# Third layer: the epsilon of the tail queries is added to their squares by VectorE, not by a one-row product on TensorE

## The reference, cut to what matters

```python
def rms_norm_2(x, g):
    xf = x.astype(jnp.float32)
    y = xf * lax.rsqrt(jnp.mean(xf * xf, axis=-1, keepdims=True) + EPS)
    return (y * g.astype(jnp.float32)).astype(x.dtype)

q, k, v, qi, ki, wi = jnp.split(h @ w_in, list(A_SPLITS), axis=-1)
q = rope(rms_norm_2(q.reshape(B, T, A_Q_HEADS, HEAD_DIM), q_gain), cos, sin)
...
score = jnp.einsum('qh,qhs->qs', w_blk, jax.nn.relu(logits))
score = jnp.where(causal, score, -jnp.inf)
_, idx = lax.top_k(score, topk)
```

## Time and profile before

| what | value |
|---|---|
| three runs, median | 1284.07 us (1283.54 to 1284.81) |
| the profiled execution | 1283.08 us |
| its span | 1281.2 us |
| TensorE busy | 1259.3 us, 98% of the span |
| VectorE busy | 808.0 us, 63% |
| ScalarE busy | 738.5 us, 58% |
| granted TensorE clock | 1.00 |

### The profile page before, as it was taken

How to read it: one execution, slowest core, us unless ns; L and a number is a source line. 1 busy time by engine, 2 the same in 40 slices (tenths; PEclk the granted TensorE clock), 3 DMA queues, 4 the chain that set the end, 5 groups by cost and what they waited for, 6 DMA issues and landing times.

```text
span 1281.2 us, 28400 instructions
## 1 busy us (share of the span) xinstructions
PE 1259.3 (98%) x10337; PEld 1214.3 (95%) x10337; DVE 808.0 (63%) x1422; ACT 738.5 (58%) x1375; POOL 375.8 (29%) x416
## 2 busy tenths in 40 slices
PE   6999999999999999999999899999999999999999
PEld 6988999999988999999989599999999889999999
DVE  5687755556576655556699875554547666755444
ACT  6566766654456566665566854443436776544433
POOL 2011344411000244431243027770100220677100
PEclk9999999999999999999999999999999999999999
DMA  7542655566654465666455046556555443655654
GB/s 263 179 136 87 190 186 183 184 208 201 214 173 154 151 195 180 193 194 207 152 183 172 11 151 182 176 172 190 172 173 180 152 139 101 194 183 182 198 189 154
DMA packets 66503, 220.55 MB, mean 172 GB/s; under 512 B 9312, under 2 KB 13808, under 8 KB 66288
## 3 DMA queue, kind: packets, MB, share of 16 engines
q1 hardware_dynamic: 64080, 212.77, 52.4%
q10 hardware_dynamic: 2336, 6.58, 1.6%
HBM read 215.61 MB, written 1.08 MB: 169 GB/s over the span
## 4 chain that ended last, share of the span: by engine, by line
PE 74%; issue 10%; DVE 5%; ACT 5%; POOL 5%; DMA 1%; POOLq 0%; ACTq 0%; SPq 0%; DVEq 0%
PE bank L341 22%; PE bank L343 22%; PE bank L342 22%; DVE wlo L325 1%; POOL scratch L581 1%; POOL scratch L583 1%; ACT prob L968 1%; ACT whi L320 1%; POOL alo L585 1%; PE bank L930 1%; DVE scratch L571 1%; ACT ahi L556 1%; PE bank L915 1%; PE bank L912 1%; PE bank L355 1%
## 5 line engine op out<-in xcount | busy, mean ns | idle before, releaser
L325 DVE TENSOR_TENSOR wlo<-raw,whi 128x1024 fp32r<-128x1024 f32 (+1 forms) x394 | 484.0, 1229 | 163.1 <-ACT whi L320 162.1
L341 PE MATMUL bank<-uhi,whi 128*128 128x256 f32 (+1 forms) x1848 | 532.6, 288 | 11.2 <-DVE wlo L325 10.2
L343 PE MATMUL bank<-uhi,wlo 128*128 128x256 f32 (+1 forms) x1848 | 524.8, 284 | 0.0
L342 PE MATMUL bank<-ulo,whi 128*128 128x256 f32 (+1 forms) x1848 | 524.0, 284 | 0.0
L320 ACT ACTIVATE whi<-raw 128x1024 fp32r<-128x1024 f32 (+1 forms) x394 | 410.6, 1045 | 184.0 <-PE bank L343 175.4
L341 PEld LDWEIGHTS bank<-uhi,whi 128*128 128x128 f32 x1848 | 349.6, 189 | 19.4 <-issue 16.7
L343 PEld LDWEIGHTS bank<-uhi,wlo 128*128 128x128 f32 x1848 | 349.9, 189 | 0.0
L342 PEld LDWEIGHTS bank<-ulo,whi 128*128 128x128 f32 x1848 | 348.4, 189 | 0.5
L341 PE MATMUL bank<-ahi,whi 128*128 128x256 f32 (+1 forms) x1168 | 332.9, 285 | 0.4 <-DVE wlo L325 0.4
L343 PE MATMUL bank<-ahi,wlo 128*128 128x256 f32 (+1 forms) x1168 | 330.6, 283 | 0.0
L342 PE MATMUL bank<-alo,whi 128*128 128x256 f32 (+1 forms) x1168 | 330.3, 283 | 0.0
(11 more groups left out here) (286 smaller groups left out, 1240.6 us busy)
## 6 DMA issues: line engine op xcount, KB each, us to landing
raw<-stream SPq DMA_DIRECT2D x394, 512.0 KB, 3.7
scratch<-decay ACTq DMA_DIRECT2D x8, 416.0 KB, 3.7
scratch<-relh ACTq DMA_DIRECT2D x8, 384.0 KB, 3.5
scratch<-scratch SPq DMA_DIRECT2D x68, 34.0 KB, 2.5
constants<-consts SPq DMA_DIRECT2D x1, 1296.0 KB, 11.4
h<-xT SPq DMA_DIRECT2D x4, 256.0 KB, 5.6
out<-h SPq DMA_DIRECT2D x8, 128.0 KB, 3.4
scratch<-scratch SPq DMA_DIRECT2D x16, 16.0 KB, 3.0
```

Of the source, the lines that this page charges most:

```text
L325: dve.tensor_tensor(wlo[:, s, 0:w], raw[:, s, 0:w], whi[:, s, 0:w].bitcast(F32), ALU.subtract).then_inc(w_lo, 1)
L341: pe.matmul(dst, hi, a, start=first and i == 0, stop=False)
L342: pe.matmul(dst, hi, b, start=False, stop=False)
L343: mm = pe.matmul(dst, lo, a, start=False, stop=last and i == chunks - 1)
```

## The change

In each of the eight dq units' statistics the one-row product L1814 is taken out, and L1813 closes the sum alone. Instead VectorE adds the scaled epsilon, spread over all 128 partitions, to the squares of the 16 tail columns in `ysq` before TensorE sums them (the matrix `headones` averages in such a way that this is the same number). This is the new function `tail_epsilon(i)`, one `tensor_tensor` of 128 x 16, with a new semaphore `y_eps`; TensorE waits for it between L1810 and L1813. On VectorE it stands in iteration i + 1 of the loop, behind `split_lo` and `second(i - 1)` and ahead of the top-k steps; for unit 19 it stands behind the first two heads' maxima. To have the number on all partitions, a product of a row of ones with the row of token factors is added once where wi is turned (`second` of wi on TensorE), one VectorE copy of 128 x 16 with it (`wi_done` now reaches 4), and the exponential L1979 works on 128 x 16 instead of 1 x 16.

```diff
                     elif name == "wi":
-                        pe.wait_ge(wi_done, 3)
+                        pe.wait_ge(wi_done, 4)
...
                     for t in range(2):
                         pe.matmul(st[:, 288 + 2 * t:290 + 2 * t], sq[:, 128 * t:128 * t + 128], const("headones")[:, 0:128:64],
                                   start=True, stop=True, skip_group_check=True)
-                    pe.wait_ge(q_eps, 2)
-                    pe.matmul(st[:, 292:308], const("headones"), sq[:, 256:T], start=True, stop=False, skip_group_check=True)
-                    pe.matmul(st[:, 292:308], ones[0:1, :], wi[0:1, 28:44], start=False, stop=True,
+                    pe.wait_ge(y_eps, j + 1)
+                    pe.matmul(st[:, 292:308], const("headones"), sq[:, 256:T], start=True, stop=True,
                               skip_group_check=True).then_inc(y_stat, 1)
...
-                        mm = pe.transpose(dsa_bank(i)[:, 24 + t:25 + t], x2_t[0:1, 2, 128 * t:128 * t + 128], const("ident")[0:1, 0:1])
-                    mm.then_inc(wi_turned, 1)
+                        pe.transpose(dsa_bank(i)[:, 24 + t:25 + t], x2_t[0:1, 2, 128 * t:128 * t + 128], const("ident")[0:1, 0:1])
+                    pe.matmul(dsa_bank(i)[:, 26:42], ones[0:1, :], x2_t[0:1, 2, 256:T], start=True, stop=True,
+                              skip_group_check=True).then_inc(wi_turned, 1)
...
-                act.activation(wi[0:1, 28:44], x2_t[0:1, 2, 256:T], ACT.Exp, bias=bias[0:1, 3:4]).then_inc(q_eps, 1)
+                act.activation(wi[:, 28:44], wi[:, 28:44], ACT.Exp, bias=bias[:, 2:3]).then_inc(q_eps, 1)
...
+            def tail_epsilon(i):
+                j, r = DSA[i][1], rms_of(i)
+                if j == 0:
+                    dve.wait_ge(q_eps, 2)
+                dve.wait_ge(y_sq, r + 1)
+                e = ysq[:, r % 2, 256:T]
+                dve.tensor_tensor(e, e, wi[:, 28:44], ALU.add).then_inc(y_eps, 1)
...
+                    dve.tensor_copy(wi[:, 28:44], dsa_bank(i)[:, 26:42]).then_inc(wi_done, 1)
...
                 if i >= 2 and DSA[i - 2][0] != "dk":
                     second(i - 2)
+                if i >= 1 and DSA[i - 1][0] == "dq":
+                    tail_epsilon(i - 1)
...
                     for i in (2 * s, 2 * s + 1):
                         biased_max_dve(dve, a, i)
+                if s == 0:
+                    tail_epsilon(19)
                 if s in (0, 4):
                     tail_max_dve(dve, s // 4)
```

More of the change, by code:

```diff
@@ L303, in program @@
         f_exp, f_log = sems("f_exp f_log")
-        q_tables, q_neg, q_eps = sems("q_tables q_neg q_eps")
+        q_tables, q_neg, q_eps, y_eps = sems("q_tables q_neg q_eps y_eps")
         t_q, t_s, t_max, t_exp, t_p, t_pt, t_pts, t_o, t_ohi, t_olo = sems(
@@ L1975, in epsilons @@
             def epsilons():
-                act.wait_ge(wi_done, 3)
+                act.wait_ge(wi_done, 4)
                 act.activation(wi[:, 26:28], wi[:, 24:26], ACT.Exp, bias=bias[:, 2:3]).then_inc(q_eps, 1)
-                act.activation(wi[0:1, 28:44], x2_t[0:1, 2, 256:T], ACT.Exp, bias=bias[0:1, 3:4]).then_inc(q_eps, 1)
+                act.activation(wi[:, 28:44], wi[:, 28:44], ACT.Exp, bias=bias[:, 2:3]).then_inc(q_eps, 1)
             for i in range(len(DSA)):
```

## The result

The changed kernel takes 1289.62 us, the median of 5 runs (1288.72 to 1291.12), against 1284.07 us before: the ratio is 1.0041, with a 95% interval of 1.0028 to 1.0054. Once more, in another session, it took 1289.83 us (10 runs) against 1284.63 us (33 runs), ratio 1.0039 (1.0026 to 1.0051). It is slower by 5.2 to 5.6 us as medians go.

A forecast was written before the change was run, and what follows sets the result against it. TensorE bounds the dq units, VectorE having 1.6 us spare in 32. Delay is +3.50 us at dq0, +4.38 through the ring, +3.52 at the next product, +4.6 after dq7: 1284.07 to 1288.7 us, range 1286.4 to 1290.8.

The forecast's parts named there:

- TensorE sets the pace: In the dq units TensorE is busy for all of 32.00 us, VectorE for 30.38; period 4.12 us, 3.80 without L1814.
- L1814's time is on the path: In the dq units, removing eight L1814 of 0.32 us takes 2.6 us off the path.
- The preparation is hidden: At wi, the additional product, some 0.3 us, fits in TensorE's 0.52 us idle time ahead of the first index product.
- VectorE reaches dq0's place over 3 us late: At dq0, TensorE reaches L1813 at 682.09, VectorE the addition's place at 685.30: a stall of over 3 us.
- X12: Start of L1813's weight load in dq0: 682.09 before, 685.59 forecast (+3.50 us).
- The ring at 4.28 us: Behind dq0, the loop L1813, L1926, L320, L325, addition, next L1813: 4.18 us plus 0.10 for each stall.
- 0.10 us for a product that starts on an idle TensorE: At each stall, a product on idle TensorE takes longer, as L1810 takes 0.61 instead of 0.50 us.
- my marks: Forecast starts of L1813's weight load by unit: 685.59 at dq0, 689.87, 694.39, 698.67, 702.95 at dq4, 710.65 at dq6.
- dq7's place costs 1.3 us: At unit 19, the addition behind L959's first two heads' maxima adds about 1.3 us, bringing the delay to +4.62 us.
- The clock stays up: At dq0's stall, the forecast counted no clock fall; the rival with a fall had chance 0.12.
- The rival's 1.7 us: Clock falls in first stall: 1.7 us more at dq1, 1.1 us stays; +5.7 us, 1289.8 us; chance 0.12.
- forecast 4.6: At the attention's start, total delay of +4.6 us, carried to the end: median 1284.07 to 1288.7 us; chance 0.60.

The follow-up runs named there:

- filler kernel: Changed kernel plus 13 float32 products of 128 x 128 constants on TensorE ahead of the wait at dq0 only: 1288.62 us, ratio 1.0031.
- Early: Changed kernel with the additions moved in VectorE's order to just behind the time their squares are there: 1282.29 us, again 1281.85 us (ratio 0.9979).
- early2: Early with dq6's and dq7's additions moved further up in VectorE's order: 1283.45 us (ratio 0.9989), again 1283.06 us (0.9987).
- one line up: Changed kernel with the addition ahead of `split_lo` in the same iteration, dq7's place kept: 1287.03 us against 1284.84, ratio 1.0007.
- late7: early2 with dq7's addition behind the first two heads' maxima, as in the change: 1283.71 us, ratio 0.9988.

## Why the prediction was right, and where it was off

- **TensorE sets the pace, and L1814's time is on the path:** right. A product's worth was 0.43 us instead of the 0.32 that I read off the chain and the weight loads, so a period paced by TensorE is 3.69 and not 3.80 us.
- **The preparation is hidden:** shown. The wider exponential takes 0.30 us, as the narrow one before took 0.29.
- **VectorE reaches dq0's place over 3 us late:** right, and the reason for the sign. Expected X12 was 685.59; less the 1.17 us of offset the profile has 685.54. The stall was 3.29 us (expected some 3.3). From the end of the addition to the waiting L1813 it is 0.06 us (686.65 to 686.71), where I had put 0.05.
- **The ring at 4.28 us:** shown. dq3 and dq4 follow at 4.29 and 4.30 us, and moving the addition past one instruction makes it 3.69. One term is right by luck. I added 0.10 us for a product that starts on an idle TensorE, read off L1810 at 709.11, but that one follows on L915 with no idle time ahead of it. In the turn of the ring above L1813 to L1926 is 0.43 us, with nothing to add, and the 0.10 us lies between the end of ScalarE's L320 and VectorE's L325 (699.62 to 699.73), where I had 0.01. In the filler kernel, where the clock doesn't fall, my marks hold: counted on the times of before, dq1 to dq4 lie at 689.84, 694.27, 698.57 and 702.87 against 689.87, 694.39, 698.67 and 702.95 predicted. Behind them it runs ahead of my sum, 710.27 against 710.65 at dq6: 0.11 us a period by the first point; it was 0.08 us ahead at dq4 already, and the 0.10 us of idle start isn't there (the period behind the last wait is 3.71 us, 0.02 over 3.69).
- **dq7's place costs 1.3 us:** 65.32 - 60.87 = 4.45 behind, after 3.13 at the tail's scores: 1.32 us.
- **The clock stays up:** this is the step that failed. I gave its fall a chance of 0.12, since no row showed a gap of that length, and a price of 1.1 us. It falls in both traces of the changed kernel, to 0.50 around gaps of 3.29 and 3.27 us, and costs 1.8 us. The rival's 1.7 us were my estimate, 17 x 0.10 us, from the kernel's start, where products follow each other 0.21 to 0.22 us apart from 10.55 to 14.18 us and 0.12 us apart later. No run shows that term behind a stall; here 21 or 22 of a unit's 24 are slow, and dq1's L1813 comes at 691.67 (692.84 less the offset) instead of the rival's 691.2. The ring then carries the delay on undiminished, where I had it shrink to 1.1 us.
- **The size:** at the turn the loss is 5.92 us, made of 4.14 us with the clock up (forecast 4.6; the product's higher worth and the idle start that isn't there explain the difference, about half each) and 1.78 us for the clock. The medians give 5.2 to 5.6 us. That the forecast, 1288.7 us, came within about 1 us of the result is in part luck: these two terms hid some 0.5 us of the missing 1.8 us for the clock.
- **By the busy shares of the whole kernel,** TensorE 98% and VectorE 63%, the sum would have been the removed products alone, -2.6 us. Early (-2.1 and -2.8 us), early2 (-1.4 and -1.6) and the additions on GpSimd (-1.9) show that they point the right way, once the engine that takes the work over is there in time; by themselves they say nothing of that.

What stays open: early's median is 1.2 us under early2's in the session that had both, its turn only 0.4 us earlier. How often the clock falls in the attention (below) may be the rest, but no run tells it apart.

## What to carry to other kernels

Before work goes from a full engine to a half-empty one, look at the time at which the other engine's queue reaches the place, not at its busy share: VectorE was 3.3 us behind TensorE here and nobody had noticed, since nothing waited. The wait that closed a ring over three engines cost 0.6 us in each turn here (4.29 us against 3.69); moving it ahead of the one instruction that closes the ring took 3.5 us off, 1.9 of them the ring's. And a stall of TensorE is dearer than its length when the clock falls in it or behind it: by 1.8 us here.

## What the hardware showed that I had not expected

- **The clock also falls in the attention, in most runs of the kernel before.** Of 103 runs of it in the three sessions, 26 have a granted clock of 1.000 and a median of 1282.9 us, 44 have 0.997 and 1285.2 us, 13 have less and 1288.5 us (the other 20 lie between 0.998 and 0.999). The profile of before happened to be one of the first kind, so where the clock falls in the others is seen in the other versions' traces alone. Each of them has a fall somewhere between 706 and 727 us, around the attention's start; the kernel with the preparation alone, which has the marks of before, has it from 715 to 722 us. In the one of the changed kernel the fall is seen behind the stretch with TensorE busy for 1.19 of 4 us, in pieces:

```profile
719.00:723.00 4.00, 1.19 (x8) 0.77 (x8) 3.44 (x18) 3.53 (x15) 0.76 (x1) 0.98 0.00 0
723.00:727.00 4.00, 4.00 (x23) 2.47 (x24) 3.93 (x23) 2.65 (x13) 0.00 (x0) 0.59 0.00 0
```

  In the same place before, the stretch from 711 to 715 us has 1.88 us busy and a clock of 1.00. From the turn to the next layer's first L341 the profile of before takes 35.13 us and that of the preparation alone 37.09. A difference of 2 us between two single profiles of this kernel may be nothing but that.
- **The clock fell in a gap of 2.49 us too** (one line up: at 684.8 us, the gap's last tenth), and with products on constants in the gap it stayed up (filler: 3.71 of 4 us busy, clock 1.00).
- **A 128 x 16 addition on VectorE took 0.75 us instead of 0.17 where it started just behind an operation of GpSimd** (703.65 and 703.61 in the rows of early2; 0.75 us also in its second trace and in late7's, 0.04 us behind the same operation), and it ended 0.02 us behind that one: 703.65 + 0.75 = 704.40 against 703.61 + 0.77 = 704.38. The other seven additions of each of these traces take 0.16 to 0.18 us. What holds the long one up, no run shows. So a small operation on VectorE wasn't always a small one here, where GpSimd was at work.
